# First modulation columns by float32r passes over weights split on chip, and the context's norm moved into the first pair of weight tiles

## The chip, the cores and the metric

The kernel runs on one core of a Trainium2 chip. The metric is the device time in microseconds (us) of one execution, the median of several. The engines of the core are named as the profile names them: PE is TensorE (matmul), DVE is VectorE, ACT is ScalarE, POOL is GpSimd, and SP is the engine whose queue issues the DMAs. SBUF is the on-chip working memory, PSUM the banks that PE writes.

## What is computed

The whole kernel is a network of four mixer layers over 512 tokens of width 1024 with a context of 256 tokens. The change touches only its first microseconds, the first norm with its modulation:

```
m_lat = (silu(c) @ ada_w[0] + ada_b[0])
m_ctx = silu(c_ctx) @ ada_w[0] + ada_b[0]
sh1, sc1, g1, sh2, sc2, g2 = split(m_lat, 6)        # likewise csh1, csc1, ... of m_ctx
h_lat = rmsnorm(x, norm_g[0, 0]) * (1.0 + sc1) + sh1
h_ctx = rmsnorm(ctx, norm_g[0, 0]) * (1.0 + csc1) + csh1
z = h @ ab_w_in[0]                                   # both, 24 tiles of 128 columns
```

Only sh1 and sc1 (the first 2048 of the 6144 columns) are needed before `z`; they are the "first modulation columns". The other 4096 come later from rows of `ada` on DVE.

## The kernel before

Matrices that must keep full precision are split into a high part, rounded to float32r, and a low part, the rest. A product is then three matmuls: high by high, low by high, high by low. Activations are split by ACT (high) and DVE (low), weights by POOL: line 297 rounds a chunk of 128x1024 (`w_hi`), line 303 subtracts (`w_lo`). A chunk is 512 KB; chunks go through four raw buffers `w_raw` in turn.

The order of the work is written by hand. The program is a list of phases, and each engine runs its part of each phase in the list's order; semaphores tie the engines together. At the start of the list stand `Load` (vectors and identity), `Start`, two `Apply` phases (latent, then context), the loads for the later rows (`ada_c`, `ada_raw`), two small tables (`p_edge`, `hmask`), and the first product, `Gemm`.

`Start` holds the first modulation columns and the two norms. The weights `ada_n` are eight tiles of 128x2048, 1 MB each, number k for rows 128k to 128k+127 of `ada_w`. SP issues tiles 0 and 1, then `x` (2 MB), tiles 2 and 3, then `xc` (the context, 1 MB), tiles 4 to 7. PE multiplies each tile with the two columns of `c_silu` in plain float32, four matmuls of 512 columns (line 1403), each shown as two records. ACT squares x and the context (lines 1423 and 1425), DVE folds the eight blocks of each with one reduction (lines 1439 and 1441), PE adds over the partitions with a matrix of ones (line 1408 after tile 4, line 1411 after tile 6), and ACT takes Ln and Exp of the sum for the reciprocal root (lines 1428 and 1429, 1431 and 1432). When the columns are done, ACT copies four rows out of PSUM (line 1435), PE turns them into columns (line 1415), DVE adds the bias and makes the gains (lines 1445 to 1449).

`Apply` then runs over eight blocks k: DVE scales (line 1027), ACT rounds to `h_hi` (line 1043), DVE subtracts to `h_lo` (line 1034). DVE issues the scaling of block k before the subtraction of block k-1. The context's `Apply` does the same with blocks of 256 columns, after the latent one.

The `Gemm` begins with its first pair of weight tiles, taken block by block as `Apply` delivers them: lines 330 to 332 for all eight latent blocks, then for all eight context blocks. The third tile follows at once, on buffers of its own (`third`), from line 388 on. From there PE works through the other tiles.

Of the kernel before, what the change touches and what calls it, by code (L numbers as in the profile page):

```python
# [77 lines left out]
def build(nc, xT, ctxT, cvec, vecs, cst, ada0n, ada0, ada1, w_ab_in, w_ab_out, w_pool, w_f0u, w_f0d, w_att_in, w_att_out,  # L78
# [4 lines left out]
    with ctx:  # L83
# [131 lines left out]
        class Side:  # L215


            def sp(self, sp, i, j): pass
            def act_first(self, act): pass
# [6 lines left out]
        class Gemm(Phase):  # L226
# [3 lines left out]
            def __init__(self, w, tiles, parts, kt, rhs, t=TL, ctx_rhs=None, ctx_from=0, evac_act=None, evac_dve=None,  # L230
                         peel=(), gate=None, gate_k=None, gate_c=None, rows=None, table=None, hi_act=False, side=None, gate_ctx=None,
                         early=None, free_k=None, third=None, first_after=0, own=(), own_after=None, ctx_pairs=False):
                super().__init__()
                self.ctx_pairs = ctx_pairs
# [28 lines left out]
            def sp(self, sp):  # L263
                def turn(i, a):
                    for j in range(RAW):
# [4 lines left out]
                        sp.dma_start(w_raw[j][:, 0:self.kt], src).then_inc(raw_ready[j], 16)  # L270
# [5 lines left out]
            def pool(self, pool):  # L276
                def turn(i, a):
                    seam = self.quad and isinstance(i, int)
                    for at_, j in enumerate((*range(SPL, RAW), *range(SPL)) if seam and i == 0 else range(RAW)):
# [4 lines left out]
                        hi, lo = self.split(i, j)  # L284
                        if seam and i == 0 and j >= SPL:
# [29 lines left out]
            def pe(self, pe):  # L315
# [5 lines left out]
                def first_pair():  # L321
# [3 lines left out]
                    for rhs, out_ in sides:  # L325
                        for k in range(self.kt):
                            hi, lo = rhs(k)
                            pe.wait_ge(*(self.gate_k if rhs is self.rhs else self.gate_c)(k))
                            for n in range(SPL):
# [3 lines left out]
                                if k == self.kt - 1 and rhs is sides[-1][0]:  # L333
                                    last.then_inc(chunk_done, 1)

# [671 lines left out]
        class Apply(Phase):  # L1007


            def __init__(self, src, nt, t, gain, shift, hi, lo, rms, gate=None, by=None, bufs=None):  # L1010
                super().__init__()
                self.by, self.bufs = rstd if by is None else by, bufs or wk
# [26 lines left out]
            def act(self, act):  # L1039
                for k in range(self.nt):  # L1040
                    act.wait_ge(self.scaled[0], self.scaled[1] + k + 1)
                    bias = self.shift(k) if self.shift else 0.0
                    sig(nc.scalar, nc.scalar.activation(self.hi(k), self.bufs[k % 2][:, 0:self.t], ACT.Identity, bias=bias), self.hi_ready)

# [325 lines left out]
        ada_row = arena("ada_row", [2, 2 * D], 32 * K)  # L1370
        x_sq = arena("x_sq", [P, ND, TL], 0)
        xc_sq = arena("xc_sq", [P, ND, TC], 16 * K)
        c_silu = arena("c_silu", [P, ND, 2], 40 * K)
        x_sum = arena("x_sum", [P, TL], 42 * K)
        xc_sum = arena("xc_sum", [P, TC], 44 * K)

        class Start(Phase):


            def __init__(self):  # L1380
                super().__init__()
                self.w_in = [cnt.take(f"row_in{k}", 16) for k in range(ND)]
                self.x_in, self.xc_in = cnt.take("x_in", 16), cnt.take("xc_in", 16)
                self.c_ready, self.sq, self.sums = cnt.take("st_c", 1), cnt.take("st_sq", 2), cnt.take("st_sums", 2)
                self.folded = cnt.take("st_folded", 2)
                self.in_ps, self.copied, self.turned = cnt.take("st_rows", 4), cnt.take("st_copied", 4), cnt.take("st_turned", 1)
# [3 lines left out]
            def sp(self, sp):  # L1390
                for k in range(ND):
                    if k == 2:
                        sp.dma_start(x[:, :, :], xT.rearrange("(k p) t -> p k t", p=P)).then_inc(self.x_in[0], 16)
                    if k == 4:
                        sp.dma_start(xc[:, :, :], ctxT.rearrange("(k p) t -> p k t", p=P)).then_inc(self.xc_in[0], 16)
                    sp.dma_start(ada_n[k][:], ada0n[k:k + 1].rearrange("o p f -> (o p) f")).then_inc(self.w_in[k][0], 16)

            def pe(self, pe):
                pe.wait_ge(*upto(self.c_ready, 1))
                for k in range(ND):  # L1400
                    pe.wait_ge(*upto(self.w_in[k], 16))
                    for q in range(4):
                        last = nc.tensor.matmul(ps[q][0:2, :], c_silu[:, k], ada_n[k][:, 512 * q:512 * q + 512], start=k == 0, stop=k == ND - 1)
                        if k == ND - 1:
                            last.then_inc(self.in_ps[0], 1)
# [3 lines left out]
                    if k == 6:  # L1409
                        pe.wait_ge(*upto(self.folded, 2))  # L1410
# [2309 lines left out]
```

## Time and profile before

| | us |
|---|---|
| median of 3 runs | 3215.86 (3213.72 to 3218.40) |
| span of the profiled execution, first to last instruction | 3209.6 |
| PE busy in it | 3102.9 (97%) |
| last record of the first modulation columns ends | 43.20 |
| `Apply` begins on DVE | 45.06 |
| first pair of weight tiles begins on PE | 47.54 |
| third tile begins on PE | 67.25 |

A line of the timeline gives a start in us from the span's start, a duration, the engine, the line of the kernel, the operation, and what it writes and reads; in brackets stands how long the engine had been idle and what released it. A group of equal instructions on one engine that follow one another is merged into one line with its count. The profile's matmul ends are modelled; two matmuls in a row overlap in their records, so that the distance of their starts is the cost of one.

### The profile page before, as it was taken

How to read it: one execution, taken by the hardware profiler on the slowest of the kernel's cores; microseconds unless marked ns; L12 is line 12 of the kernel's file. 1: busy time of each engine (PE TensorE's matmuls, PEld its weight loads, DVE VectorE, ACT ScalarE, POOL GpSimd, SP SyncE). 2: the span in 40 equal slices, each digit the busy share in tenths (PEclk: the TensorE clock that was granted, in tenths of full speed). 3: DMA queues.
4: the chain of work that ended last, by engine and by line, in shares of the span. 5: the costliest groups of instructions: out<-in, count | busy, mean ns of one | idle time of the engine just before them, and what ended most of it. 6: DMA issues, size and time to landing. Idle time of an engine off the chain costs nothing.

```text
span 3209.6 us, 40755 instructions
## 1 busy us (share of the span) xinstructions
PE 3102.9 (97%) x15496; PEld 2574.5 (80%) x15496; DVE 1610.5 (50%) x2488; ACT 948.9 (30%) x1707; POOL 1653.3 (52%) x880
## 2 busy tenths in 40 slices
PE   8998889999999998999999999999999999999998
PEld 4887777888999766888878888788888788888887
DVE  4897668712332775211157667435531456645521
ACT  3124431111353463111023355322211214632210
POOL 2441045666787404566646633466665663066664
PEclk9999999999999999999999999999999999999999
DMA  5531026632454201233222311233232221023231
GB/s 225 191 119 44 14 82 244 236 118 88 146 182 152 66 7 66 72 98 107 100 72 92 96 43 40 70 95 98 93 109 89 92 93 67 14 92 94 96 109 68
DMA packets 84552, 319.29 MB, mean 99 GB/s; under 512 B 9200, under 2 KB 10864, under 8 KB 83376
## 3 DMA queue, kind: packets, MB, share of 16 engines
q1 hardware_dynamic: 84400, 317.20, 29.7%
q8 instruction: 103, 1.69, 0.2%
q14 instruction: 49, 0.40, 0.0%
HBM read 315.06 MB, written 2.10 MB: 99 GB/s over the span
## 4 chain that ended last, share of the span: by engine, by line
PE 83%; DVE 8%; issue 3%; ACT 2%; DMA 2%; POOL 1%; SPq 0%; DVEq 0%; POOLq 0%; ACTq 0%
PE two L388 15%; PE two L390 15%; PE two L389 15%; PE two L537 7%; PE two L539 7%; PE two L538 7%; DMA ada_raw<-ada 2%; PE two L2459 1%; DVE ada_junk L1120 1%; PE two L3059 1%; PE two L1728 1%; PE two L3061 1%; PE two L2594 1%; PE two L3060 1%; PE two L2619 1%
## 5 line engine op out<-in xcount | busy, mean ns | idle before, releaser
L388 PE MATMUL two<-h_hi,w_hi 128*128 128x512 f32 x2096 | 825.0, 394 | 4.4 <-DVE hid_lo L2110 3.4
L390 PE MATMUL two<-h_hi,w_lo 128*128 128x512 f32 x2096 | 816.4, 390 | 0.0
L389 PE MATMUL two<-h_lo,w_hi 128*128 128x512 f32 x2000 | 778.9, 389 | 0.0
L303 POOL TENSOR_TENSOR w_lo<-w_raw,w_hi 128x1024 fp32r<-128x1024 f32 x292 | 712.7, 2442 | 40.7 <-ACT w_hi L414 11.7
L297 POOL TENSOR_SCALAR w_hi<-w_raw 128x1024 fp32r<-128x1024 f32 x272 | 290.6, 1069 | 671.9 <-issue 331.8
L388 PEld LDWEIGHTS two<-h_hi,w_hi 128*128 128x128 f32 x2096 | 394.0, 188 | 90.7 <-issue 3.9
L390 PEld LDWEIGHTS two<-h_hi,w_lo 128*128 128x128 f32 x2096 | 393.8, 188 | 82.6
L389 PEld LDWEIGHTS two<-h_lo,w_hi 128*128 128x128 f32 x2000 | 376.0, 188 | 77.9 <-issue 1.4
L505 POOL TENSOR_SCALAR w_hi<-w_raw 128x1408 fp32r<-128x1408 f32 (+1 forms) x105 | 133.5, 1271 | 518.1 <-PE two L539 399.7
L509 POOL TENSOR_TENSOR w_lo<-w_raw,w_hi 128x1408 fp32r<-128x1408 f32 (+1 forms) x111 | 329.1, 2966 | 40.1 <-DVE z L2222 16.5
L537 PE MATMUL two<-hid_hi,w_hi 128*128 128x512 f32 x704 | 274.1, 389 | 0.0
L539 PE MATMUL two<-hid_hi,w_lo 128*128 128x512 f32 x704 | 273.9, 389 | 0.0
L538 PE MATMUL two<-hid_lo,w_hi 128*128 128x512 f32 x704 | 273.9, 389 | 0.0
L2108 DVE TENSOR_TENSOR two<-wk,two 128x512 f32<-128x512 f32 (+1 forms) x66 | 40.0, 606 | 303.6 <-PE two L390 268.0
L3379 DVE SCALAR_TENSOR_TENSOR wk<-two,vec,wk 128x511 f32<-128x511 f32 (+1 forms) x176 | 131.9, 750 | 97.9 <-ACT wk L3357 85.2
L538 PEld LDWEIGHTS two<-hid_lo,w_hi 128*128 128x128 f32 x704 | 132.2, 188 | 27.6
L539 PEld LDWEIGHTS two<-hid_hi,w_lo 128*128 128x128 f32 x704 | 132.2, 188 | 27.4
L537 PEld LDWEIGHTS two<-hid_hi,w_hi 128*128 128x128 f32 x704 | 132.2, 188 | 27.3
L1120 DVE SCALAR_TENSOR_TENSOR ada_junk<-ada_raw,ada_c 128x1024 f32<-128x1024 f32 x64 | 108.3, 1745 | 20.1 <-DMA ada_raw<-ada 20.1
L3357 ACT ACTIVATE wk<-two,vec 128x512 f32<-128x512 f32 x88 | 60.7, 690 | 164.5 <-DVE two L3373 164.5
L3373 DVE TENSOR_TENSOR two<-two,rstd 128x512 f32<-128x512 f32 x88 | 61.2, 695 | 95.8 <-PE two L390 95.8
L2100 ACT CAST hid_hi<-two 128x512 fp32r<-128x512 f32 (+1 forms) x44 | 25.8, 587 | 264.9 <-DVE two L2108 264.9
(625 smaller groups left out, 5701.9 us busy)
## 6 DMA issues: line engine op xcount, KB each, us to landing
w_raw<-w_f0u SPq DMA_DIRECT2D x88, 512.0 KB, 3.5
row_raw<-ada SPq DMA_DIRECT2D x48, 512.0 KB, 5.0
w_raw<-w_ssm SPq DMA_DIRECT2D x48, 512.0 KB, 3.5
w_raw<-w_f0d SPq DMA_DIRECT2D x32, 704.0 KB, 4.0
w_raw<-w_f1u SPq DMA_DIRECT2D x44, 512.0 KB, 3.5
w_raw<-w_f2u SPq DMA_DIRECT2D x44, 512.0 KB, 3.5
w_raw<-w_f3u SPq DMA_DIRECT2D x44, 512.0 KB, 3.5
ada_raw<-ada SPq DMA_DIRECT2D x32, 512.0 KB, 3.7
```

What stands on the lines that cost most here:

```text
L297: nc.gpsimd.tensor_scalar(hi[:, 0:self.kt], w_raw[j][:, 0:self.kt], 1.0, 1.0, ALU.mult, ALU.mult).then_inc(hi_done, 1)
L303: nc.gpsimd.tensor_tensor(lo[:, 0:self.kt], w_raw[j][:, 0:self.kt], hi[:, 0:self.kt].bitcast(f32), ALU.subtract).then_inc(split_done, 1)
L388: nc.tensor.matmul(dst, w_h[:, k], hi, start=kk == 0, stop=False)
L389: nc.tensor.matmul(dst, w_h[:, k], lo, start=False, stop=False)
L390: last = nc.tensor.matmul(dst, w_l[:, k], hi, start=False, stop=kk == self.parts * self.kt - 1)
L505: nc.gpsimd.tensor_scalar(hi, raw, 1.0, 1.0, ALU.mult, ALU.mult).then_inc(hi_done, 1)
L509: nc.gpsimd.tensor_tensor(lo, raw, hi.bitcast(f32), ALU.subtract).then_inc(split_done, 1)
L537: nc.tensor.matmul(self.out(t), w_h[:, k], hi, start=kk == 0, stop=False)
L538: nc.tensor.matmul(self.out(t), w_h[:, k], lo, start=False, stop=False)
L539: last = nc.tensor.matmul(self.out(t), w_l[:, k], hi, start=False, stop=kk == self.parts * self.kt - 1)
L1120: nc.vector.scalar_tensor_tensor(self.bufs.junk[v][:], self.bufs.raw[j][:], 1.0, self.bufs.c[:, v], ALU.mult, ALU.mult, accum_out=mods[sel ...
L3379: nc.vector.scalar_tensor_tensor(wk[n][:, back:TL], g.out(n)[:, 0:TL - back], self.col(i, n, j), wk[n][:, back:TL], ALU.mult, ALU.add).the ...
```

## The change

It does these things at the start and nothing after the first pair:

- The first modulation columns are made in float32r. ACT rounds each 512 columns of a weight tile into `ada_hi` (six buffers in turn, 32 casts in all), DVE subtracts into `ada_lo` in the tile's own place (32 subtractions), and PE multiplies both by `c_four`, four columns: the high and low part of the two `c_silu` columns. The turning into columns adds the high and low rows in the same matmul, with a small matrix of zeros and ones, `row_pair`.
- DVE folds the squares of x by three additions (2048, 1024 and 512 columns) in place of the reduction, after the pieces of tile 3. PE's sum for x stands after tile 5, and ACT's copy, Ln and Exp of it stand after the casts of tile 5 and before those of tile 6.
- DMA order: `ada_n` 0 to 2, x, 3 to 6, the first weight chunk of the first product, 7, the second chunk, then the context. In the `Gemm` these two chunks are no longer issued.
- The context's norm: ACT squares it after its part of the row copies and before its first `h_hi`. POOL folds it with three additions between the splits of chunks 1 and 2. PE's sum for it stands in the first pair after block 4, ACT's Ln and Exp after `h_hi` of block 5.
- Two of the four row copies go to DVE.

ACT, in `Start`. Before, it had nothing to do for the weights; the norm's chain stood between the squares and the row copies:

```order
L1423 ACTIVATE x_sq<-x 128x4096 [waits x_in]
L1425 ACTIVATE xc_sq<-xc 128x2048 [waits xc_in]
L1427 COPY x_sum_103<-two 128x512 [waits st_sums]
L1428 ACTIVATE two<-two,epsv 128x512 [waits act_step]
L1429 ACTIVATE two<-two 128x512 [waits act_step]
L1431 ACTIVATE two<-two,epsv 128x256 [waits st_sums,rstd_ready]
```

Now, at the end of tile 5 (`ada_n_128`) and the beginning of tile 6 (`ada_n_129`):

```order
L1469 CAST ada_hi_144<-ada_n_128 128x512 [waits row_used]
L1479 COPY x_sum_103<-two 128x512 [waits st_sums]
L1480 ACTIVATE two<-two,epsv 128x512
L1481 ACTIVATE two<-two 128x512 [waits act_step]
L1469 CAST ada_hi_139<-ada_n_129 128x512 [waits row_used,row_in6]
L1469 CAST ada_hi_140<-ada_n_129 128x512 [waits row_used]
```

The wait for the sum now stands in front of the casts of tiles 6 and 7.

POOL, the first chunks. Before:

```order
L297 TENSOR_SCALAR w_hi_53<-w_raw_49 128x1024
L303 TENSOR_TENSOR w_lo_55<-w_raw_49,w_hi_53 128x1024 [waits hi_done]
L297 TENSOR_SCALAR w_hi_54<-w_raw_50 128x1024 [waits raw_ready1,chunk_done]
L303 TENSOR_TENSOR w_lo_56<-w_raw_50,w_hi_54 128x1024 [waits hi_done]
L297 TENSOR_SCALAR third_hi<-w_raw_51 128x1024 [waits raw_ready2,chunk_done]
```

Now:

```order
L303 TENSOR_SCALAR w_hi_53<-w_raw_49 128x1024
L309 TENSOR_TENSOR w_lo_55<-w_raw_49,w_hi_53 128x1024 [waits hi_done]
L303 TENSOR_SCALAR w_hi_54<-w_raw_50 128x1024 [waits raw_ready1,chunk_done]
L309 TENSOR_TENSOR w_lo_56<-w_raw_50,w_hi_54 128x1024 [waits hi_done]
L1449 TENSOR_TENSOR xc_sq<-xc_sq 128x1024 [waits c_sq,raw_ready2]
L1449 TENSOR_TENSOR xc_sq<-xc_sq 128x512 [waits lc_folded]
L1449 TENSOR_TENSOR xc_sq<-xc_sq 128x256 [waits lc_folded]
L303 TENSOR_SCALAR third_hi<-w_raw_51 128x1024 [waits lc_folded,chunk_done]
```

The four instructions of the first two splits are the same and wait for the same; three additions now stand before the third split.

ACT, in `Apply`. Before:

```order
L1435 COPY ada_row<-two 2x512 [waits st_rows,c_rstd]
L1435 COPY ada_row<-two 2x512 [waits st_rows] x3
L1043 ACTIVATE h_hi<-two,mods_62 128x512 [waits scaled]
L1043 ACTIVATE h_hi<-two,mods_62 128x512 [waits scaled,h_hi_ready] x7
L1043 ACTIVATE c_hi<-two,mods_62 128x256 [waits scaled,h_hi_ready] x8
```

Now:

```order
L1484 COPY ada_row<-two 4x512 [waits row_used] x2
L1486 ACTIVATE xc_sq<-xc 128x2048 [waits xc_in]
L1052 ACTIVATE h_hi<-two,mods_62 128x512 [waits scaled]
L1052 ACTIVATE h_hi<-two,mods_62 128x512 [waits scaled,h_hi_ready] x5
L1454 ACTIVATE two<-two,epsv 128x256 [waits c_sum,h_hi_ready]
L1455 ACTIVATE two<-two 128x256 [waits act_step]
L1052 ACTIVATE h_hi<-two,mods_62 128x512 [waits scaled]
```

The context's chain moved from ahead of the row copies into the middle of the latent `h_hi`, with a wait for PE's sum in front of block 6.

The diff, cut to its core (`rounded(k)` is ACT's four casts of tile k, from the seventh piece on each behind PE's last use of its buffer):

```diff
             def sp(self, sp):
+                def chunk(j):
+                    sp.dma_start(w_raw[j][:, 0:8], self.w[j:j + 1].rearrange("o p k f -> (o p) k f")).then_inc(raw_ready[j], 16)
                 for k in range(ND):
-                    if k == 2:
+                    if k == 3:
                         sp.dma_start(x[:, :, :], xT.rearrange("(k p) t -> p k t", p=P)).then_inc(self.x_in[0], 16)
-                    if k == 4:
-                        sp.dma_start(xc[:, :, :], ctxT.rearrange("(k p) t -> p k t", p=P)).then_inc(self.xc_in[0], 16)
+                    if k == ND - 1:
+                        chunk(0)
                     sp.dma_start(ada_n[k][:], ada0n[k:k + 1].rearrange("o p f -> (o p) f")).then_inc(self.w_in[k][0], 16)
+                chunk(1)
+                sp.dma_start(xc[:, :, :], ctxT.rearrange("(k p) t -> p k t", p=P)).then_inc(self.xc_in[0], 16)
...
                 for k in range(ND):
-                    pe.wait_ge(*upto(self.w_in[k], 16))
                     for q in range(4):
-                        last = nc.tensor.matmul(ps[q][0:2, :], c_silu[:, k], ada_n[k][:, 512 * q:512 * q + 512], start=k == 0, stop=k == ND - 1)
+                        p, cols = 4 * k + q, slice(512 * q, 512 * q + 512)
+                        pe.wait_ge(*upto(self.hi, p + 1))
+                        nc.tensor.matmul(ps[q][0:4, :], c_four[:, k], ada_hi[p % 6][:], start=k == 0, stop=False)
+                        pe.wait_ge(*upto(self.lo, p + 1))
+                        nc.tensor.matmul(ps[q][0:4, :], c_four[:, k], ada_lo[k][:, cols], start=False, stop=k == ND - 1).then_inc(self.used[0], 1)
-                    if k == 4:
+                    if k == 5:
                         pe.wait_ge(*upto(self.folded, 1))
-                        nc.tensor.matmul(ps[6][:], ones[:], x_sum[:], start=True, stop=True).then_inc(self.sums[0], 1)
+                        nc.tensor.matmul(ps[6][:], ones[:], x_sq[:, 0], start=True, stop=True).then_inc(self.summed[0], 1)
...
+                for k in range(ND):
+                    rounded(k)
+                    if k == 2:
+                        act.wait_ge(*upto(self.x_in, 16))
+                        for i in range(2):
+                            nc.scalar.activation(x_sq[:, 4 * i:4 * i + 4], x[:, 4 * i:4 * i + 4], ACT.Square, scale=1.0 / 32).then_inc(self.sq[0], 1)
+                    if k == 5:
+                        act.wait_ge(*upto(self.summed, 1))
+                        nc.scalar.copy(x_sum2[:], ps[6][:])
+                        astep(nc.scalar.activation(ps[6][:], ps[6][:], ACT.Ln, bias=epsv[:, 0:1]))
+                        nc.scalar.activation(ps[6][:], ps[6][:], ACT.Exp, scale=-0.5).then_inc(self.rstd[0], 1)
...
+                        dve.wait_ge(*upto(self.hi, p + 1))
+                        nc.vector.tensor_tensor(ada_lo[k][:, cols], ada_n[k][:, cols], ada_hi[p % 6][:].bitcast(f32), ALU.subtract).then_inc(self.lo[0], 1)
+                    if k == 3:
+                        dve.wait_ge(*upto(self.sq, 2))
+                        vstep(nc.vector.tensor_tensor(x_sq[:, 0:4], x_sq[:, 0:4], x_sq[:, 4:8], ALU.add))
+                        vstep(nc.vector.tensor_tensor(x_sq[:, 0:2], x_sq[:, 0:2], x_sq[:, 2:4], ALU.add))
+                        nc.vector.tensor_tensor(x_sq[:, 0], x_sq[:, 0], x_sq[:, 1], ALU.add).then_inc(self.folded[0], 1)
```

## Rows read from the trace of the kernel before

**Rows 1.** Timeline of PE, start: us, duration, engine, line, operation, tiles, [idle, releaser]

```profile
8.66 9.16 PE L1403 MATMUL two<-ada_n,c_silu 128*2 128x512 f32 x16 [8.66 <-DMA ada_n<-ada0n]
19.45 7.03 PE L1403 MATMUL two<-ada_n,c_silu 128*2 128x512 f32 x16 [1.64 <-DMA ada_n<-ada0n]
27.44 3.59 PE L1403 MATMUL two<-ada_n,c_silu 128*2 128x512 f32 x8 [0.96 <-DMA ada_n<-ada0n]
30.96 1.13 PE L1408 MATMUL two<-x_sum,ones 128*128 128x512 f32 x2
...
39.61 3.59 PE L1403 MATMUL two<-ada_n,c_silu 128*2 128x512 f32 x8
43.13 1.16 PE L1415 MATMUL two<-ident,ada_row 2*128 2x2 f32 x16
47.54 0.76 PE L330 MATMUL two<-h_hi,w_hi 128*128 128x512 f32 x1 [3.25 <-DVE h_lo L1034]
...
55.85 0.39 PE L330 MATMUL two<-h_hi,w_hi 128*128 128x512 f32 x1
...
67.25 0.40 PE L388 MATMUL two<-h_hi,third_hi 128*128 128x512 f32 x1
```

**Rows 2.** Timeline of DVE, from the bias to the end of the latent blocks

```profile
44.33 0.27 DVE L1445 TENSOR_TENSOR two<-two,vec 128x16 f32<-128x16 f32 x2 [12.88 <-PE two L1415]
...
45.06 1.54 DVE L1027 SCALAR_TENSOR_TENSOR two<-x,gains,two 128x512 f32<-128x512 f32 x2
...
56.12 1.60 DVE L1034 SCALAR_TENSOR_TENSOR h_lo<-two,mods,h_hi 128x512 fp32r<-128x512 f32 x2
```

**Rows 3.** Timeline of ACT, the norm of x and the latent block 6

```profile
16.97 3.62 ACT L1423 ACTIVATE x_sq<-x 128x4096 f32<-128x4096 f32 x1 [11.51 <-DMA x<-xT]
...
32.13 0.58 ACT L1427 COPY x_sum<-two 128x512 f32<-128x512 f32 x1 [5.28 <-PE two L1408]
32.74 0.66 ACT L1428 ACTIVATE two<-two,epsv 128x512 f32<-128x512 f32 x1
33.44 0.58 ACT L1429 ACTIVATE two<-two 128x512 f32<-128x512 f32 x1
...
54.59 0.69 ACT L1043 ACTIVATE h_hi<-two,mods 128x512 fp32r<-128x512 f32 x1 [0.89 <-DVE two L1027]
```

**Rows 4.** Timeline of POOL, the splits of the first two chunks

```profile
40.05 1.04 POOL L297 TENSOR_SCALAR w_hi<-w_raw 128x1024 fp32r<-128x1024 f32 x1 [39.60 <-DMA w_raw<-w_ab_in]
...
44.62 2.34 POOL L303 TENSOR_TENSOR w_lo<-w_raw,w_hi 128x1024 fp32r<-128x1024 f32 x1
```

**Rows 5.** Instructions of one line, DVE and ACT: count, ns min/median/max, first and last start

```profile
L2235 DVE TENSOR_TENSOR z_lo<-z,q_hi x8: 678/685/693, 1113.9 to 1197.6; 128x512 fp32r<-128x512 f32 x8
...
L2226 ACT CAST q_hi<-z x8: 602/608/609, 1111.6 to 1194.4; 128x512 fp32r<-128x512 f32 x8
```

**Rows 6.** Groups of DVE by line and form: count | busy us, mean ns | idle before

```profile
L2668 DVE TENSOR_TENSOR d_p<-d_p,d_col 128x1024 f32<-128x1024 f32 x16 | 19.6, 1225 | 0.6
```

**Rows 7.** Timeline of DVE, two additions in a row with no wait between

```profile
446.00 0.69 DVE L787 TENSOR_TENSOR e_buf<-e_buf,e_buf 128x512 f32<-128x512 f32 x1
446.61 0.68 DVE L801 TENSOR_TENSOR e_buf<-e_buf,e_buf 128x512 f32<-128x512 f32 x1
```

**Rows 8.** Timeline of DVE and POOL where both read SBUF

```profile
78.71 2.40 POOL L303 TENSOR_TENSOR w_lo<-w_raw,w_hi 128x1024 fp32r<-128x1024 f32 x1
79.11 3.07 DVE L1120 SCALAR_TENSOR_TENSOR ada_junk<-ada_raw,ada_c 128x1024 f32<-128x1024 f32 x1 [1.39 <-DMA ada_raw<-ada]
...
82.12 1.22 DVE L1120 SCALAR_TENSOR_TENSOR ada_junk<-ada_raw,ada_c 128x1024 f32<-128x1024 f32 x1
...
210.47 1.80 POOL L297 TENSOR_SCALAR w_hi<-w_raw 128x1024 fp32r<-128x1024 f32 x1 [4.81 <-issue]
```

**Rows 9.** Stretches: busy us of each engine, PE's granted clock, DMA share, GB/s

```profile
43.70:47.10 3.40, 0.59 (x10) 0.51 (x8) 2.63 (x9) 1.20 (x3) 3.32 (x3) 1.00 0.61 213
47.10:50.50 3.40, 2.96 (x7) 2.41 (x8) 3.26 (x5) 1.62 (x3) 3.25 (x2) 0.50 0.02 5
```

More of the change, by code:

```diff
@@ L218, in sp, with pool, pe_first @@
             def sp(self, sp, i, j): pass
+            def pool(self, pool): pass
+            def pe_first(self, pe, k): pass
             def act_first(self, act): pass
@@ L1396, in sp, with turn @@
                     sp.dma_start(ada_n[k][:], ada0n[k:k + 1].rearrange("o p f -> (o p) f")).then_inc(self.w_in[k][0], 16)
+                chunk(1)
+                sp.dma_start(xc[:, :, :], ctxT.rearrange("(k p) t -> p k t", p=P)).then_inc(self.xc_in[0], 16)
             def pe(self, pe):
-                pe.wait_ge(*upto(self.c_ready, 1))
+                pe.wait_ge(*upto(self.c_ready, 2))
+                def turn(q):
+                    pe.wait_ge(*(upto(self.copied, q + 1) if q < 2 else upto(self.dve_copied, q - 1)))
+                    for n in range(4 * q, 4 * q + 4):
+                        last = nc.tensor.matmul(ps[4][:, 2 * n:2 * n + 2], ada_row[:, n * P:(n + 1) * P], row_pair, start=n == 0, stop=True, skip_group_check=True)
+                    return last
@@ L1409, in pe @@
-                    if k == 6:
-                        pe.wait_ge(*upto(self.folded, 2))
-                        nc.tensor.matmul(ps[7][:, 0:TC], ones[:], xc_sum[:], start=True, stop=True).then_inc(self.sums[0], 1)
+                        nc.tensor.matmul(ps[6][:], ones[:], x_sq[:, 0], start=True, stop=True).then_inc(self.summed[0], 1)
                 for q in range(4):
-                    pe.wait_ge(*upto(self.copied, q + 1))
-                    for n in range(4 * q, 4 * q + 4):
-                        last = nc.tensor.transpose(ps[4][:, 2 * n:2 * n + 2], ada_row[:, n * P:(n + 1) * P], ident[0:2, 0:2])
+                    last = turn(q)
@@ L1416, in pe, with ctx_sum, pool_fold @@
                 last.then_inc(self.turned[0], 1)
+            def ctx_sum(self, pe):
+                pe.wait_ge(*upto(self.c_folded, 3))
+                nc.tensor.matmul(ps[7][:, 0:TC], ones[:], xc_sq[:, 0], start=True, stop=True).then_inc(self.c_summed[0], 1)
+            def pool_fold(self, pool):
+                pool.wait_ge(*upto(self.xc_squared, 1))
+                for i, n in enumerate((4, 2, 1)):
+                    nc.gpsimd.tensor_tensor(xc_sq[:, 0:n], xc_sq[:, 0:n], xc_sq[:, n:2 * n], ALU.add).then_inc(self.c_folded[0], 1)
+                    pool.wait_ge(*upto(self.c_folded, i + 1))
@@ L1428, in act @@
-                astep(nc.scalar.activation(ps[6][:], ps[6][:], ACT.Ln, bias=epsv[:, 0:1]))
-                sig(nc.scalar, nc.scalar.activation(ps[6][:], ps[6][:], ACT.Exp, scale=-0.5), self.rstd)
-                act.wait_ge(*upto(self.sums, 2))
-                astep(nc.scalar.activation(ps[7][:, 0:TC], ps[7][:, 0:TC], ACT.Ln, bias=epsv[:, 0:1]))
-                sig(nc.scalar, nc.scalar.activation(ps[7][:, 0:TC], ps[7][:, 0:TC], ACT.Exp, scale=-0.5), self.rstd_c)
-                for q in range(4):
-                    act.wait_ge(*upto(self.in_ps, q + 1))
-                    nc.scalar.copy(ada_row[:, 512 * q:512 * q + 512], ps[q][0:2, :]).then_inc(self.copied[0], 1)
```

90 lines of the change are left out of this document (62 added, 28 removed).

## The prediction

> **What bounds the kernel now.** I read the page first, for how little of the span the change can reach, and then the timeline of each engine over the first 70 us. Everything from the third tile on, which begins at 67.25 [rows 1], is left as it is: PE is what works there, and the third tile and its followers depend on the start only through the moment at which they may begin. So the question is by how much that row moves. Before it stand three stretches. The first is the columns: PE's first matmul waits 8.66 us for a weight tile, then PE follows the transfers, waiting for them three times, the last time at 27.44, and from there on its own pace sets the end: the last three tiles are through at 39.61 + 3.59 = 43.20 [rows 1]. The second is the tail from there to the first scaling of `Apply` at 45.06 [rows 2], 1.86 us of copying, turning and bias. The third is `Apply` with the first pair, from 45.06 to 67.25, or 22.19 us, in which DVE gives a latent block about every 1.58 us and PE follows; the last latent subtraction ends at 57.72 [rows 2], and the context blocks take the rest, 9.5 us.
>
> **When the transfers land.** Five MB of the same transfers are ahead of 19.45 in both orders: PE's second stretch begins there, released by tile 2 [rows 1]. From 27.44 (tile 4) to 40.05 (chunk 0, which POOL waited for [rows 4]) another 4.9 MB came, 2.57 us for each MB. By that pace, in the new order: tile 2 at about 14, x at about 19.4, tile 3 at 22, tiles 4 to 6 at 24.5, 27.1 and 29.7, chunk 0 at 31.0, tile 7 at 33.5, chunk 1 at 34.8, the context at 37.4. So the transfers would let the columns end some six us earlier than now. The question is whether ACT, DVE and PE keep up.
>
> **The new columns, step by step.** PE now waits for pieces of 512 columns that ACT and DVE prepare, so the work moves to them: 32 subtractions. A subtraction of this form, both inputs in SBUF, takes 0.685 us, a cast on ACT 0.608 [rows 5], and two DVE additions with no wait between them start 0.61 apart [rows 7]. A tile costs DVE 4 x 0.61 = 2.44 us, hardly less than its transfer, so DVE catches up nothing that it once loses, and steps 1 to 4 all lose.
> 1. The squares. ACT does them before the casts of tile 3, from x's landing at 19.4, 3.62 us [rows 3], in two halves some 3.7: 23.1. The first cast gives DVE its first piece at 23.7, its four pieces end at 26.2.
> 2. The fold of x, now behind tile 3. An addition of 1024 takes 1.225 [rows 6], 512 takes 0.685 [rows 5], by the same slope 2048 takes 2.3: together 4.2 us, to 30.4. The old reduction was longer, but lay in DVE's idle time.
> 3. Tiles 4 and 5, eight pieces: 4.9 us, to 35.3, if nothing were in the way. POOL is in the way. Its two instructions for a chunk take 1.04 and 2.34 [rows 4], and the chunks land at 31.0 and 34.8, in the middle of this. Where POOL and DVE both read SBUF, one waits for the other: with POOL's subtraction running from 78.71 to 81.11, DVE's instruction took 3.07 against 1.22 alone, and where DVE was first, POOL's rounding took 1.80 in place of 1.04 [rows 8]. In this trace they take turns, and a DVE stream is held up by each POOL instruction for its length. That is 2 x (1.04 + 2.34) = 6.8 us, to 42.1. Before, DVE was idle during these splits, or read PSUM in one operand.
> 4. The norm of x. PE's sum comes after tile 5's last piece: 0.4 for that matmul and 1.13 for the sum [rows 1]; then ACT's 0.58 + 0.66 + 0.58 [rows 3], 1.9 with the hops, then the first cast of tile 6, 0.6. DVE has nothing to do meanwhile and goes on at 46.1. This is the new wait: behind ACT's wait for the sum are queued all eight casts of tiles 6 and 7, and behind those DVE and PE. Tile 7 has then been in SBUF for 12 us.
> 5. Tiles 6 and 7, eight pieces: 4.9 us, to 51.0; the last matmuls 0.4; the tail as before 1.86, with half the copies on DVE, which I count as nothing. `Apply` would begin at 53.3.
>
> **PE's clock.** After its idle stretch of 3.25 us PE ran at a granted clock of 0.50, the 1.2 GHz level, from 47.10 to 50.50 [rows 9]. In steps 3 to 5 PE is idle for longer than that more than once, so I expect that level there in part: the sum then costs about 1.1 more, and matmuls of some 0.42 (seven took 2.96 in that stretch), 0.85 for a piece, slower than DVE's 0.61, up to 2 us over eight pieces. Between 0 and 3, I take 0.7, since the level will not be low all the time: `Apply` begins at 54.0, that is 8.9 us later than now.
>
> *A rule weighed.* The starts of two additions lie 0.61 us apart while each lasts 0.69 [rows 7]. The Trainium skill (VectorE: DVE Perf Modes, The DRAIN you can't avoid) says that the next op does not start until the pipe of the one before is empty. By it the twenty pieces of steps 1, 3 and 5 would cost 0.08 us more each, and `Apply` would begin 1.6 us later still; by the rows nothing is added, and I go by the rows.
>
> **Apply and the first pair.** Two changes here. ACT squares the context (half of 3.62 and a fixed part, about 1.9) after its two row copies and before its first `h_hi`: the context has landed long since, and the tail of 1.86 plus the first scaling covers it, so nothing; had it landed late, it would cost up to 1.9. POOL's folding of the context (1024, 512 and 256 columns, some 4.3 us by its 2.34 for 1024 [rows 4]) lies beside it and beside the first blocks, whose DVE instructions read PSUM; nothing. It is done before PE reaches block 4's end, and the third chunk's split behind it has until the third tile: nothing. What costs is the wait that ACT makes after block 5. PE was through with block 4 at 55.85 [rows 1], 10.8 us after `Apply` began; the context's sum, half of 1.13, then Ln and Exp of 256 columns, some 0.9 by the wide ones [rows 3], come to 57.4 on the old clock, while `h_hi` of block 6 began at 54.59 [rows 3]. So block 6 comes 2.9 us late; with blocks 6 and 7 back to back after it, the last subtraction ends some 2.1 later than 57.72. The context blocks wait for that, on DVE, and end 2.1 later too. Bounds: 1 if PE is not slow at the pair's start, 3 if nothing is made up.
>
> **Sum.** +8.9 + 2.1 = +11.0 us, the row of 67.25 moving to about 78. The profiled execution has a span of 3209.6, which gives 3220.6; the median lies 6.3 above that span, so 3215.9 + 11.0 = 3226.9.
>
> **The rivals.**
> *POOL yields.* If a DVE stream in fact keeps POOL out, so that POOL gets in only while DVE waits for the norm of x (4 us, enough for one split), the 6.8 us of step 3 are mostly gone: +4.2, 3220.1. For it: few rows show the turn-taking with a full DVE stream. Against it: POOL's rounding at 210.47 took only 0.76 longer than alone, about one DVE instruction [rows 8].
> *The transfers bound.* The change would do what its form suggests if DVE owed nothing when tile 7 lands at 33.5: cast 0.6, four pieces 2.4, matmul 0.4, tail 1.9, `Apply` at 38.8, 6.3 earlier; the wait in `Apply` takes 2.1 back: -4.2, 3211.7. This is the case that is not slower. It is decided by DVE's debt at 33.5: it needs that the casts, the fold and the splits hold up nothing, and by steps 1 and 2 alone DVE is then still on tile 5.
> *PE bounds.* If the granted clock stays at the lower level through tiles 4 to 7, PE's 0.85 us a piece replaces 0.61 for sixteen pieces, 4 us in place of the 0.7 above: +14.3, 3230.2. It decides once pieces come faster than every 0.85.
> *The change doesn't do what it says:* that the context's chain is cheap inside the pair. That is in the forecast already, as +2.1.
>
> **How the numbers follow.** My forecast, 0.68; POOL yields, 0.16; the transfers bound, 0.06; PE bounds, 0.10. The likeliest case gives 3226.9. Its own bounds, 0 to 3 for the clock and 1 to 3 for the wait, give 3225 to 3230. The range reaches down to 3219, which takes in the case where POOL yields, and up to 3231, which takes in PE. About 0.2%, 6.4 us, is what a measurement of this kernel can tell from no change: slower than 3222.3 are the forecast and PE's case, less a little for sums that are too long, 0.75; between 3209.4 and 3222.3 lie POOL's case, most of the transfers' case and that little, 0.22; faster, 0.03, needs the transfers' case without the wait in `Apply`.
>
> **What would show it.** In the profile of the changed kernel: DVE's subtractions of tile 3 begin at 23 to 24; three additions of x up to about 30; four DVE records of 1.5 to 3 us beside POOL's four; a DVE gap of some 4 us before tile 6, released by ACT; the first scaling near 54 (46 if POOL yields and the clock is high, 39 if the transfers bound); an ACT wait of 2 to 3 us before `h_hi` of block 6; the third tile near 78. The prediction is wrong if DVE's subtractions beside POOL stay at 0.69, if the casts of tile 6 come before the norm's end, or if the stretch behind the third tile changes its length.

## The result: slower by 0.5%, and by more than predicted

| | before | changed |
|---|---|---|
| median of the times | 3214.79 (3213.43 to 3218.40) | 3231.76 (3229.32 to 3234.04) |
| ratio, with its 95% interval | | 1.0052 (1.0040 to 1.0064) |
| span of the profiled execution | 3209.6 | 3232.3 |
| `Apply` begins on DVE | 45.06 | 58.30 |
| last latent subtraction ends | 57.72 | 73.99 |
| third tile begins on PE | 67.25 | 83.52 |

The change costs 17 us. The direction was forecast, the size was not: 3226.9 was the value, 3231.0 the upper end of the range. The third tile comes 16.3 us later in place of 11.0.

DVE's timeline of the changed kernel, in the columns of [rows 2]:

```profile
23.60 2.50 DVE L1496 TENSOR_TENSOR ada_lo<-ada_n,ada_hi 128x512 fp32r<-128x512 f32 x4 [6.68 <-ACT ada_hi L1469]
26.01 2.28 DVE L1499 TENSOR_TENSOR x_sq<-x_sq 128x2048 f32<-128x2048 f32 x1
28.33 1.23 DVE L1500 TENSOR_TENSOR x_sq<-x_sq 128x1024 f32<-128x1024 f32 x1
29.59 0.69 DVE L1501 TENSOR_TENSOR x_sq<-x_sq 128x512 f32<-128x512 f32 x1
30.20 10.90 DVE L1496 TENSOR_TENSOR ada_lo<-ada_n,ada_hi 128x512 fp32r<-128x512 f32 x8
46.31 4.90 DVE L1496 TENSOR_TENSOR ada_lo<-ada_n,ada_hi 128x512 fp32r<-128x512 f32 x8 [5.21 <-ACT ada_hi L1469]
52.74 1.28 DVE L1504 COPY ada_row<-two 4x512 f32<-4x512 f32 x2 [1.53 <-PE two L1434]
57.57 0.26 DVE L1508 TENSOR_TENSOR two<-two,vec 128x16 f32<-128x16 f32 x2 [3.56 <-PE two L1425]
...
58.30 1.55 DVE L1036 SCALAR_TENSOR_TENSOR two<-x,gains,two 128x512 f32<-128x512 f32 x2
...
72.45 1.54 DVE L1043 SCALAR_TENSOR_TENSOR h_lo<-two,mods,h_hi 128x512 fp32r<-128x512 f32 x2 [3.13 <-ACT h_hi L1052]
```

Read it downwards as the prediction's steps. Eight pieces take 4.90 us where nothing is in the way and 10.90 where POOL splits. POOL's four instructions beside them, against 1.04 and 2.34 [rows 4]:

```profile
30.84 1.55 POOL L303 TENSOR_SCALAR w_hi<-w_raw 128x1024 fp32r<-128x1024 f32 x1 [30.39 <-DMA w_raw<-w_ab_in]
32.48 2.66 POOL L309 TENSOR_TENSOR w_lo<-w_raw,w_hi 128x1024 fp32r<-128x1024 f32 x1
35.12 1.48 POOL L303 TENSOR_SCALAR w_hi<-w_raw 128x1024 fp32r<-128x1024 f32 x1
36.68 2.67 POOL L309 TENSOR_TENSOR w_lo<-w_raw,w_hi 128x1024 fp32r<-128x1024 f32 x1
```

PE's timeline, from the sum for x on; [rows 1] has the same steps before:

```profile
42.04 1.91 PE L1437 MATMUL two<-x_sq,ones 128*128 128x512 f32 x2
46.33 0.59 PE L1432 MATMUL two<-ada_hi,c_four 128*4 128x512 f32 x1 [2.38 <-ACT ada_hi L1469]
...
53.09 4.44 PE L1425 MATMUL two<-small,ada_row 4*128 4x2 f32 x32
60.78 0.76 PE L336 MATMUL two<-h_hi,w_hi 128*128 128x512 f32 x1 [3.25 <-DVE h_lo L1043]
...
70.21 0.60 PE L1444 MATMUL two<-xc_sq,ones 128*128 128x256 f32 x2
...
83.52 0.40 PE L396 MATMUL two<-h_hi,third_hi 128*128 128x512 f32 x1
```

The row at 53.09 is the one that the prediction did not have: the turning, in 32 records and 4.44 us, where [rows 1] has 16 records and 1.16 us. The granted clock, in the columns of [rows 9]:

```profile
32.00:52.00 20.00, 12.77 (x27) 2.86 (x27) 14.00 (x14) 7.12 (x14) 7.18 (x4) 0.50 0.73 274
52.00:56.00 4.00, 4.00 (x30) 3.12 (x28) 1.28 (x2) 2.33 (x2) 1.52 (x1) 0.93 0.01 4
56.00:64.00 8.00, 4.75 (x16) 4.01 (x16) 6.11 (x14) 2.75 (x4) 6.22 (x5) 0.50 0.00 1
```

PE is at 0.50, the 1.2 GHz level, for the whole stretch from the splits to the last products, and again when the first pair begins.

**The two spans are 22.7 us apart, the medians 17.0.** Of the 6.4 us by which the spans differ beyond the third tile's 16.3, 5.3 arise in a later stage in which PE often pauses: from the third tile's start to the second product's third tile it is 396.7 us in this profile of before and 402.0 in the changed kernel's. A second profile of the kernel before shows 404.0 there, so this is scatter of the executions. Three profiles, over 136 us of that stretch (before, before profiled a second time, changed; the column ahead of the DMA share is the mean granted clock):

```profile
248.00:384.00 136.00, 111.81 (x799) 100.10 (x798) 104.52 (x204) 65.24 (x96) 10.33 (x6) 0.99 0.09 30
```

```profile
248.00:384.00 136.00, 111.95 (x754) 100.84 (x753) 104.95 (x204) 63.12 (x93) 10.35 (x6) 0.91 0.09 30
```

```profile
264.00:400.00 136.00, 113.28 (x771) 101.85 (x770) 103.88 (x204) 63.02 (x93) 10.33 (x6) 0.92 0.09 30
```

The same kernel before shows 0.99 once and 0.91 once. So effects are read below from the third tile's start, which is sharper than the time.

### The profile page after: what moved, and what is told of

Its sections match the earlier page's. It is cut to its first block, busy times and chain, and to the rows that moved or that the text cites. A ratio compares the mean times of both kernels' runs of the same rounds, so it can differ in the third digit from the quotient of the medians.

```text
span 3232.3 us, 40864 instructions
## 1 busy us (share of the span) xinstructions
PE 3111.6 (96%) x15512; PEld 2586.8 (80%) x15512; DVE 1632.8 (51%) x2525; ACT 965.9 (30%) x1739; POOL 1659.4 (51%) x883
## 4 chain that ended last, share of the span: by engine, by line
PE 83%; DVE 8%; issue 3%; ACT 2%; DMA 2%; POOL 1%; SPq 0%; DVEq 0%; POOLq 0%; ACTq 0%
PE two L396 15%; PE two L398 15%; PE two L397 15%; PE two L545 7%; PE two L547 7%; PE two L546 7%; DMA ada_raw<-ada 2%; PE two L2531 1%; DVE ada_junk L1131 1%; PE two L1800 1%; PE two L3131 1%; PE two L3133 1%; PE two L3132 1%; PE two L2666 1%; PE two L2691 1%
```

## The experiments

All times of starts are of DVE's and PE's timelines; "earlier" and "later" are against the changed kernel, if nothing else is said. A piece is one subtraction of 512 columns on DVE. In the changed kernel and its variants the first piece of tile 3 starts between 23.60 and 24.29 from run to run (24.86 in the one variant that loads a chunk ahead of x), an offset that moves everything behind it; where it matters it is named.

**The turning by transposes.** ACT's and DVE's row copies stay; DVE adds the high and low columns afterwards.

```diff
-last = nc.tensor.matmul(ps[4][:, 2 * n:2 * n + 2], ada_row[:, n * P:(n + 1) * P], row_pair, ...)
+last = nc.tensor.transpose(ps[4][:, 4 * n:4 * n + 4], ada_row[:, n * P:(n + 1) * P], ident[0:4, 0:4])
```

> The changed kernel, with the 16 turning matmuls (4 rows by a 4x2 matrix, 32 records, 4.44 us after the last product) put back to 16 transposes, which give four columns each; DVE adds the high and low columns. Everything else as in the changed kernel, where Apply begins at 58.30 and the third tile at 83.52. My theory (the tail grew because each plain float32 matmul of the turning costs two records of about 0.14 us and each loads its 4x128 weights anew, in place of one record of 0.07): the turning takes 1.2 to 1.5 us, one more DVE step 0.2, so Apply begins at about 55.5 and the third tile at about 80.7; the kernel about 2.8 us quicker, 3229. The rival (the turning is slow because PE's clock had fallen): the transposes also take about twice their 1.16 of before, 2.3 or more, and the third tile comes at 81.7 or later.

Measured: ratio 1.0055 (1.0038 to 1.0071) to before, third tile at 81.43, 2.8 earlier when its first piece, 0.69 late, is allowed for. PE's and DVE's rows:

```profile
52.32 1.38 PE L1425 MATMUL two<-ident,ada_row 4*128 4x4 f32 x16
```

```profile
54.03 0.26 DVE L1511 TENSOR_TENSOR mods<-two,mods 128x16 f32<-128x16 f32 x2
54.32 2.17 DVE L1514 SCALAR_TENSOR_TENSOR gains<-mods,vec 128x8 f32<-128x8 f32 x2
```

The turning takes 1.38, as my theory said, and not 2.3. In this run PE's clock was also back at 1.00 for the last pieces, which is not the edit's doing, since nothing ahead of the turning was changed; so the turning followed DVE's last piece by 0.4 us in place of 1.9. With both, `Apply` should begin 4.5 earlier, and it does so by 2.5 (56.52, with the late first piece): two DVE instructions of 8 columns take 2.17 us, because in this version both their inputs are in SBUF and POOL is folding the context at that moment. In the changed kernel the same two read PSUM and take 0.17 and 0.15 beside the same POOL work, and in the run with four edits below, where they read PSUM again beside a split on POOL, they take 0.17 and 0.16; the first of them:

```profile
43.69 0.17 DVE L1518 SCALAR_TENSOR_TENSOR gains<-two,vec 128x8 f32<-128x8 f32 x1
```

So a part of the gain was lost because POOL held DVE up, at a place that I had not thought of.

**The same form of turning, in the kernel before.**

```diff
-last = nc.tensor.transpose(ps[4][:, 2 * n:2 * n + 2], ada_row[:, n * P:(n + 1) * P], ident[0:2, 0:2])
+last = nc.tensor.matmul(ps[4][:, 2 * n:2 * n + 2], ada_row[:, n * P:(n + 1) * P], ident[0:2, 0:2], start=n == 0, ...)
```

> The kernel before, with its 16 transposes written as 16 plain float32 matmuls by a 2x2 identity; nothing else. My theory (the form of the turning costs, 32 records and weight loads of 0.12 to 0.14 us in place of 16 of about 0.07, whatever the kernel around it): the turning takes 3.7 to 4.5 us in place of 1.2, Apply begins at 47.7 to 48.4 in place of 45.06 to 45.24, and the third tile at 69.9 to 70.8. The rival (the turning was long in the changed kernel because four rows of PSUM copies on two engines reach PE late, or because of its clock): it stays under 2 us here.

Measured: `Apply` at 48.46, third tile at 70.64, 3.4 and 3.2 later than in the two profiles of before; ratio 1.0011 (1.0001 to 1.0020).

```profile
40.43 3.59 PE L1403 MATMUL two<-ada_n,c_silu 128*2 128x512 f32 x8
43.96 3.73 PE L1415 MATMUL two<-ident,ada_row 2*128 2x2 f32 x32
```

Not all of this is the edit: the last columns already start 0.8 late, at 40.43 in place of 39.61 [rows 1], as do ACT's squares of x (17.76 in place of 16.97 [rows 3]). From the turning's start to `Apply` it is 4.50 us in place of 1.93. So the form of the turning alone costs 2.6 us, 3.73 in place of 1.16, at a granted clock of 1.00 in both, with two rows, all copies on ACT, and none of the new columns; the rival's 2 us is out. With the offset taken off, `Apply` and the third tile come just ahead of the stretches expected for them. In the changed kernel the price is 3.3, 4.44 in place of 1.16: there the clock was at 0.98 up to 56.00 and at 0.50 for the last 1.5 us of the turning, and the other 0.7 goes with that.

**POOL's splits behind DVE's last piece.** One wait is added on POOL, ahead of its first rounding.

```diff
+pool.wait_ge(*upto(self.start.lo, 4 * ND))
```

> The changed kernel, with one wait added on POOL: its first rounding of a weight chunk waits for DVE's last subtraction of the first modulation columns. The chunks are still loaded early. My theory (POOL and DVE take turns at SBUF, so that POOL's four instructions held DVE's stream up by their full 6.8 us): DVE's eight pieces of tiles 4 and 5 take 4.9 us in place of 10.9 and everything behind comes 6 us earlier, Apply at about 52.3; the splits then run from about 46 to 53 beside the tail and give the first pair its weights at about 53, so nothing is lost there; third tile at about 77.5, kernel about 6 us quicker, 3226. The rival (DVE was not held by POOL but by ACT's casts or PE's slow clock behind the six buffers): DVE's pieces of tiles 4 and 5 still take over 9 us, and the third tile stays at 83 or later.

Measured: ratio 1.0033 (1.0020 to 1.0045), third tile at 74.73, 8.8 earlier, or 9.4 with its first piece, 0.56 late, allowed for. DVE and PE:

```profile
30.76 4.90 DVE L1499 TENSOR_TENSOR ada_lo<-ada_n,ada_hi 128x512 fp32r<-128x512 f32 x8
40.44 4.90 DVE L1499 TENSOR_TENSOR ada_lo<-ada_n,ada_hi 128x512 fp32r<-128x512 f32 x8 [4.78 <-ACT ada_hi L1472]
```

```profile
37.06 1.02 PE L1440 MATMUL two<-x_sq,ones 128*128 128x512 f32 x2
...
45.72 3.73 PE L1428 MATMUL two<-small,ada_row 4*128 4x2 f32 x32
```

The eight pieces take 4.90 in place of 10.90: POOL's splits held DVE up for 6.0 us, and ACT and PE were not the reason. The other 3.4 us come with PE's clock: without DVE's pauses PE recovered before the sum (1.02 in place of 1.91), the turning followed DVE's last piece by 0.4 in place of 1.9, and the turning took 3.73 in place of 4.44. The waits for the norm and inside `Apply` shrank with it, from 5.21 to 4.78 and from 3.13 to 2.44. Of the whole price of the early splits, 9.4 us in this kernel, about a third was paid on PE; that the clock is what made PE slow there is tested below, in the run with PE kept busy. The Trainium skill (SBUF — State Buffer, SBUF: two separate sides) has the pair of ports that DVE and POOL share as an exclusive lock, held for a whole instruction, taken by a DVE instruction with two SBUF inputs against a POOL instruction that reads SBUF. The rows agree, in the main: 6.0 us for four POOL instructions that take 6.8 here with DVE's stream out of the way, and the 2.17 above against 0.17 with an input in PSUM.

**The norm of x at the end of the casts.**

```diff
-                    if k == 5:
+                    if k == ND - 1:
                         act.wait_ge(*upto(self.summed, 1))
```

> The changed kernel, with ACT's copy, Ln and Exp of the sum for x moved from behind the casts of tile 5 to behind the casts of tile 7; PE's sum stays after tile 5. My theory (ACT's wait for the sum holds the casts of tiles 6 and 7, and DVE behind them, 5.2 us): the gap of 5.21 before tile 6 goes, except for the 1.9 us of PE's sum at the lower clock, during which up to six pieces can be cast ahead; DVE's last piece ends at about 46.5 instead of 51.2, Apply begins at about 54, third tile at about 79.2, kernel about 4.3 us quicker. The rival (PE at the lower clock, 0.85 us a piece and 1.9 for the sum, is the bound as soon as DVE no longer waits): PE goes on from 44 with eight pieces of 0.85, ends at 50.8, so only 2.3 us are gained, third tile at about 81.2.

Measured: ratio 1.0043 (1.0026 to 1.0059), third tile at 77.64, 5.9 earlier; the expectation was 4.3, the rival's 2.3.

```profile
30.22 15.71 DVE L1496 TENSOR_TENSOR ada_lo<-ada_n,ada_hi 128x512 fp32r<-128x512 f32 x16
46.64 1.28 DVE L1504 COPY ada_row<-two 4x512 f32<-4x512 f32 x2 [0.72 <-PE two L1434]
```

The sixteen pieces have no gap, and the last ends at 45.93: the wait was worth its full 5.3 us. PE, given work without a pause, returned to a clock of 1.00 during the sum (1.31 us) and kept up with DVE, so it did not bound.

**The context's Ln and Exp at the end of the latent blocks.** `inside={5: st.ctx_rstd}` becomes `inside={7: st.ctx_rstd}`.

> The changed kernel, with ACT's Ln and Exp for the context moved from behind h_hi of block 5 to behind h_hi of block 7; PE's sum for the context stays after block 4 of the first pair. My theory (ACT waits 3.96 us for the sum with blocks 6 and 7 queued behind it): blocks 6 and 7 come 1.58 apart as the others, the last latent subtraction ends 12.7 after the beginning of Apply instead of 15.7; the sum is ready at 70.8, Ln and Exp end at about 71.8, so the context follows without a wait or with one under 1 us; third tile 2.3 to 3.0 earlier, at about 80.9. The rival (PE, at the lower clock for five blocks, is the bound there and the wait on ACT only shows it): PE is done with the latent blocks at the same time as now, 76.1, and the third tile does not move by more than 1 us.

Measured: ratio 1.0038 (1.0024 to 1.0052), third tile at 81.33, 2.2 earlier. The last latent subtraction ends 12.65 after the beginning of `Apply` (12.66 before, 15.69 in the changed kernel), and 0.85 of the 3.0 comes back as a wait for the context's root. The rival is out; PE had in fact been at the lower level for two blocks only.

**PE kept busy.** Repeated products whose results nobody uses fill PE's pauses.

```diff
+                def idle(k, n):
+                    for _ in range(n):
+                        nc.tensor.matmul(ps[7][0:4, :], c_four[:, k], ada_lo[k][:, 0:512], start=True, stop=True)
```

> The changed kernel with PE kept busy: repeated float32r matmuls of 512 columns into an unused bank, 20 after tile 2, 2 beside each piece of tiles 4 and 5, 14 after tile 3, 8 after the sum for x, 12 after the turning. Their results aren't used. My theory (PE's lower clock from about 24 to 52 and from 56 to 66 costs some of the 16.3 us: 0.9 in the sum, 1.5 in the last pieces, 0.7 in the turning, and about 1.5 in the wait inside Apply): with the granted clock at 1.00 from 30 on, Apply begins at about 55.5, the last latent subtraction ends 14.2 to 15 after it, the third tile starts at 79 to 80, and the kernel gains 3.5 to 4.5 us. The rival (the clock costs nothing, since DVE's stream is the bound and PE's lag is absorbed in its waits): third tile at 82.5 or later.

Measured: third tile at 81.03, with a first piece 0.59 late, so 3.1 earlier in the chain; the 79 to 80 that I expected is missed by 1.0, by 0.4 with the late piece allowed for. In the times it doesn't show: 3231.39, ratio 1.0053 (1.0037 to 1.0068). The sum took 1.02 and the turning followed DVE's last piece by 0.4. But the clock did not hold:

```profile
52.00:56.00 4.00, 4.00 (x29) 3.98 (x29) 0.12 (x1) 0.60 (x1) 3.17 (x2) 0.73 0.00 0
56.00:60.00 4.00, 4.00 (x11) 1.19 (x11) 3.69 (x11) 1.38 (x2) 3.62 (x4) 0.50 0.00 0
```

PE had been at 1.00 from 44 to 52; then it ran the turning's 32 small records back to back, and the granted clock fell during them. The twelve products behind the turning then ran at the lower level until 60.88 and held the first pair, whose `h_lo` had been there at 59.2. So at least about 3 of the 16.3 us are the clock's. More is not shown, and not excluded either: the turning, 4.75 us, was 1.0 longer than at full clock (3.73 above), and the added products themselves kept the pair waiting for some 1.6 us.

**Four of the edits together** (transposes, splits late, both norms late; the sum of high and low is now left in PSUM, so that the gains read PSUM).

> The changed kernel with four edits together: the turning by transposes, POOL's first rounding behind DVE's last subtraction, ACT's copy, Ln and Exp for x behind the casts of tile 7, and the context's Ln and Exp behind h_hi of block 7. By the chain (third tile at 83.52; each edit alone gave 2.1, 8.8, 5.9 and 2.2): were they to add up, 19.0 earlier, 64.5. My theory says a bit less, since POOL's splits, which now begin only when DVE ends at about 40.5, end at about 47.3 and then bound the first pair, and since ACT's chain for x now stands before its row copies: Apply at about 44, third tile at 66 to 67.5, as in the kernel before (67.25), and its time within 2 us of it. The rival (one of the four terms was a symptom of another, so that the gains overlap by more than 4 us): third tile at 69 or later.

Measured: `Apply` at 44.13, third tile at 68.15, ratio 1.0000 (0.9991 to 1.0010). With them the time no longer shows a cost of the change; the third tile is still 0.9 and 0.7 later than in the two profiles of before, and misses the expected 66 to 67.5 by 0.7. The four edits alone sum to 19.0, together they give 15.4, 3.6 less. Two waits show where a part of it went, in PE's and DVE's rows:

```profile
47.41 0.77 PE L339 MATMUL two<-h_hi,w_hi 128*128 128x512 f32 x1 [4.35 <-POOL w_lo L312]
```

```profile
58.72 1.01 DVE L1039 SCALAR_TENSOR_TENSOR two<-xc,gains,two 128x256 f32<-128x256 f32 x2 [1.94 <-ACT two L1458]
```

POOL's late split holds the pair for 0.8 us, and the context's sum behind block 4 comes late with it. The starts of `Apply` split the 3.6. Before it, the edits alone gain 15.1 and together 14.2, 1.0 less. From it to the third tile, they gain 3.8 alone and 1.2 together, 2.6 less: the wait of 1.94 was 0.85 in the run with the context's norm late alone, which is 1.1, and the other three runs had each shortened the old wait inside `Apply`, by 0.3, 0.7 and 0.5, which can't be gained again once that wait is gone, 1.5. The 1.0 ahead of `Apply` is what is left of larger terms. PE's lag behind DVE's last piece, 1.9 in the changed kernel, was 0.4, 0.4 and 1.3 in three of the single runs and is 1.4 here: 3.2 less won. Against that, the run with the transposes had lost 1.8 more to POOL, and the single runs 1.2 more to late first pieces; 0.8 are in DVE's stream and the turning. That the lag is PE's clock is an argument only.

**PE sums the squares of x.** ACT writes the squares rounded to float32r, and PE adds the eight blocks; DVE's three additions go.

```diff
+                    if k == 3:
+                        pe.wait_ge(*upto(self.sq, 2))
+                        for b in range(ND):
+                            last = nc.tensor.matmul(ps[6][:], ones_r[:], x_sqr[:, b], start=b == 0, stop=b == ND - 1)
```

> As the one with four edits, and the fold of x's squares taken from DVE: ACT writes them in float32r, PE adds all eight blocks with a float32r matrix of ones after tile 3, and ACT's copy, Ln and Exp stand behind the casts of tile 6, where ACT waits for tile 7's transfer anyway. My theory (DVE's stream is the bound, so its 4.2 us of additions come off): DVE's twenty pieces run from 23.7 without a gap to about 36, Apply begins at 39 to 41, the third tile at 61.5 to 63.5, 4 to 6 us before that of the kernel before; the time about 3210, quicker than both kernels. The rival (PE at the lower clock: eight sums of 0.43 and pieces of 0.85 from 23.7 on keep it behind DVE to the end): the last product ends at 42 or later and the third tile comes at 65 or later.

Measured: `Apply` at 40.54, 4.6 ahead of the kernel before, as expected; third tile at 65.85, which I had at 61.5 to 63.5; ratio 0.9996 (0.9987 to 1.0005). The last product started at 37.88, so the rival's reason (PE behind DVE) is wrong although its number, 65, came true. PE's and DVE's rows name the two waits that took over:

```profile
44.94 0.77 PE L339 MATMUL two<-h_hi,w_hi 128*128 128x512 f32 x1 [5.46 <-POOL w_lo L312]
```

```profile
56.40 1.01 DVE L1039 SCALAR_TENSOR_TENSOR two<-xc,gains,two 128x256 f32<-128x256 f32 x2 [3.20 <-ACT two L1461]
```

POOL, kept off DVE's stream, finishes the second chunk only at 44.84 and holds the pair by 2; PE's sum for the context, behind block 4 of that pair, makes DVE wait 3.20.

**Both waits taken out:** chunk 0 is loaded ahead of x and split while DVE waits for x's squares; PE sums the context's squares right after the turning.

> As the one with x's squares summed on PE, with three more edits: the first weight chunk is loaded ahead of x, and POOL splits it at once, while DVE waits for the squares of x; only the second chunk's split waits for DVE's last subtraction; and ACT writes the context's squares in float32r too, PE sums them right after the turning, and the context's Ln and Exp stand behind h_hi of block 3. There, POOL's second chunk had ended at 44.8 and held the first pair, and the context's sum behind block 4 held DVE for 3.20 us; third tile at 65.85. My theory (only these two waits were left): Apply at 40.5 to 41.5, the pair begins 2.4 after it, no DVE wait before the context, third tile 22.2 after Apply, at 62.7 to 63.7, some 4 us before the kernel before (67.25 and 67.44), time 3209 to 3212. The rival (the chunk in front of x costs its 1.3 us of transfer time in full, and PE at the lower clock can't make up in the pair): Apply at 42 or later, or more than 23.5 from Apply to the third tile, third tile at 65 or later.

Measured: `Apply` at 41.88, third tile 22.19 later, at 64.07, 3.2 and 3.4 ahead of the two profiles of the kernel before, and 0.4 behind what I had expected. `Apply` comes 1.3 later than in the run before this one (41.88 and 40.54), as the rival has it for the chunk in front of x; its 65 for the third tile did not come. In the time it can't be told from no change: 3214.53 against 3215.44, ratio 0.9999 (0.9990 to 1.0008). Some 3 us are within the scatter of these executions, in which the kernel before ranges from 3210.5 to 3219.2.

**The kernel before, again,** for the scatter.

> The kernel before, unchanged, for a second profile. In the five profiles so far of the changed kernel and its variants the stretch from the third tile's start to the first matmul of the second product's third tile (at 463.9 before, 485.5 after) lasted 401.6 to 402.4 us, in the one profile of before 396.65; in it PE's granted clock falls for some stretches of 4 us after idle PE. If that is an accident of the execution, this profile shows 398 to 403, and the span 3211 to 3216. If the change causes it (something left behind in the later stages), this profile shows 396 to 397 again.

Measured: third tile at 67.44, the second product's third tile at 471.4, a stretch of 404.0 in place of 396.7, and 1.0 more than the 403 that I had as the upper end for an accident; span 3217.4; ratio 0.9997 (0.9988 to 1.0006). An accident of the execution, then, not something left behind by the change.

## Why the prediction was right and where it failed

| step | predicted | measured |
|---|---|---|
| 1, 2: fold of x ends | 30.4 | 30.2 |
| 3: tiles 4 and 5 end | 42.1 | 41.1 |
| 4: DVE goes on | 46.1 | 46.3 |
| 5: last piece ends | 51.0 | 51.2 |
| 5: turning begins | 52.1 with the clock's 0.7 | 53.1 |
| 5: from there to `Apply` | 1.9 | 5.2 |
| `Apply` begins | 54.0 | 58.3 |
| from there to the last latent subtraction | 12.7 + 2.1 | 15.7 |
| third tile | about 78 | 83.5 |

**Steps 1 to 4 held, the last by some luck.** The squares and the fold came within 0.2. The turn-taking of POOL and DVE, read from two rows [rows 8], cost 6.0 where I had 6.8, and the run with the splits moved confirms the cause. The norm's wait came to 5.2 in the trace and 5.3 by taking it away, where I had 4.0: PE reached the sum late and took 1.91 for it at the lower clock, not 1.13. The two errors nearly cancel, so that DVE went on at 46.3 against 46.1. The rule weighed would have added 0.08 to a piece; eight took 4.90, 0.61 each, and the rows were right.

**The step that failed is the tail of step 5, "the tail as before 1.86".** I took the new turning as a renamed old one. It is another operation: a plain float32 matmul is two records in the profile, as every float32 matmul in [rows 1] shows (8 matmuls, 16 records), and each record of the turning has a weight load of its own (32, in the last section), while the transposes are 16 records for 16. The diff shows the form, and the row of 1.16 us x16 [rows 1] shows what was replaced. The measured price is 3.3 us, 4.44 in place of 1.16, three quarters of the 4.3 us by which `Apply` was missed. Of it 2.6 are the form, by the run with only this edit in the kernel before (3.73 in place of 1.16), and 0.7 go with the clock, which fell during the turning. With these 2.6 in the sum the forecast would have been 3229.5, and the median inside a range moved up by as much.

**Two terms were too small.** The clock ahead of the turning: I took 0.7 from a range of 0 to 3, and PE was 1.9 behind DVE, 0.4 of it the usual distance, so 1.5; with the 0.8 in the sum and the 0.7 in the turning that is 3.0, the upper end of my bounds. I had argued that the level would not be low all the time; it was 0.50 from 32 to 52, where POOL's splits give PE pauses of up to 1.75 us between pieces. And the wait in `Apply`: 3.0 in place of 2.1, the upper end of its bounds, since PE did the first two blocks of the pair at the lower level.

**The base was wrong but did no harm.** I read "the median lies 6.3 above the span" as work around the span. An execution's time lies only some 1.8 above its own span (3234.04 and 3232.3); by that the profiled execution of before took 3211.4 and was a quick one. The sum was added to the median, 3214.8 in the later count, and 16.3 on it gives 3231.1 against 3231.76 measured.

**The rivals.** That POOL yields is refuted, as is that the transfers bound: tile 7 was issued by 13.96 and no tile took more than 19.7 us to land, and the casts of tiles 6 and 7 began at 45.66. PE bounded only in the weak form above. The median lies 0.8 us above the range, because the new term stood in none of the cases.

## What to carry over

Cost a replaced instruction by its form, not by its role: count the records and weight loads of the new form from a row of the same kind, above all where many tiny instructions stand on the path. A DVE stream with both inputs in SBUF beside POOL work cost nearly POOL's length here, 6.0 of 6.8 us, and 3.4 more on PE, whose clock stayed low with the pauses. Where a change adds waits in several queues, find them by moving each alone; but expect the next one right behind (here POOL's split and the context's sum), and read small effects at the first row that the change can reach, since the time of one execution of this kernel scatters by several us.

## What the hardware showed that I had not expected

- A plain float32 matmul of 4 rows by 2 columns costs 0.23 us at full clock (3.73 for 16), and 0.28 to 0.31 in the runs in which the clock fell on the way (4.44 to 4.95 for 16). A transpose of 4 by 4 costs 0.07 (twelve weight loads in 0.82; the 1.27 to 1.38 for 16 take in a wait for the last row copy). The weight loads fill the time, here in the changed kernel, 4.4 of 4.44 us:

```profile
L1425 PEld LDWEIGHTS two<-small,ada_row 4*128 4x128 f32 x32 | 4.4, 216 | 0.5 <-issue 0.5
```

- PE's granted clock fell from 1.00 to 0.50, the 1.2 GHz level, while PE ran such records without a pause (the run with PE kept busy: 1.00 from 48 to 52, 0.73 as the mean of 52 to 56, 0.50 from 56 to 60).
- DVE instructions of 8 columns can wait 2 us for POOL: 2.17 for two of them beside POOL's additions, at most 0.17 each with one input in PSUM.
